# Decoder step with sparse attention: TensorE's order around its waits in the sample stage, and who copies and pads

## The reference

```python
# per sample: 2048 past rows of k and v, 4 kv heads of 64, 4 query heads per kv head, 4 tokens
kc, vc = compress(rows)                      # blocks of 32 rows, stride 16, through a small MLP; keys normed + rotary
s_c = einsum('qhgd,nhd->hgqn', q, kc)        # scores against the 127 compressed blocks
p_c = masked_softmax(s_c);  o_c = p_c @ vc
imp = p_c @ overlap                          # importance of each block of 64 rows
top = top_k(imp + forced, 16)                # the blocks each head and token may read
p_s = masked_softmax(q @ k_sel, top);  o_s = p_s @ v_sel        # 2048 selected-branch rows
p_w = masked_softmax(q @ k_win);       o_w = p_w @ v_win        # last 512 rows
o   = g_c * o_c + g_s * o_s + g_w * o_w
```

## Time and profile before

| | |
|---|---|
| Median of three runs | 2348.47 us (2348.05 to 2349.93) |
| The profiled execution | 2348.25 us, span 2346.6 us |
| TensorE busy, whole span | 2095.6 us (89%) |
| Sample stage | 1676 to 2268 us of the span, 592 us |
| TensorE busy in the sample stage | 494.51 us, mean granted clock 0.90 |
| One sample, second and third | 72.72 and 74.01 us |

### The profile page before, as it was taken

How to read it: one execution, slowest core, us unless ns; L and a number is a source line. 1 busy time by engine, 2 the same in 40 slices (tenths; PEclk the granted TensorE clock), 3 DMA queues, 4 the chain that set the end, 5 groups by cost and what they waited for, 6 DMA issues and landing times. The chain is left out here.

```text
span 2346.6 us, 25998 instructions
## 1 busy us (share of the span) xinstructions
PE 2095.6 (89%) x9553; PEld 1219.1 (52%) x9553; DVE 730.6 (31%) x1535; ACT 480.8 (20%) x1063; POOL 213.9 (9%) x325
## 2 busy tenths in 40 slices
PE   6998999999999999889899986787788887888878
PEld 3225545554664654468533675454454554545547
DVE  2012323322323232301213404555343233432342
ACT  1111211211121121100200122444322222222220
POOL 0000010010010001000000001323310101101000
PEclk9998999999999999889999987878889988899889
DMA  6862362343146136242122543000223442233420
GB/s 177 277 217 108 125 225 83 125 168 137 73 180 214 39 137 228 102 156 71 36 72 55 150 153 118 1 1 1 90 100 133 161 161 89 98 134 161 126 73 38
DMA packets 118889, 281.22 MB, mean 120 GB/s; under 512 B 33112, under 2 KB 41758, under 8 KB 115335
## 3 DMA queue, kind: packets, MB, share of 16 engines
q1 hardware_dynamic: 100636, 170.56, 22.0%
q0 software_dynamic: 12928, 109.54, 11.6%
q10 hardware_dynamic: 5268, 0.36, 0.2%
HBM read 227.78 MB, written 60.86 MB: 123 GB/s over the span
## 5 line engine op out<-in xcount | busy, mean ns | idle before, releaser
L1483 PE MATMUL sample_bank<-area 128*128 128x508 f32 x512 | 221.3, 590 | 0.0
L1296 PE MATMUL proj_bank<-stage,area 128*128 128x512 f32 (+1 forms) x400 | 175.6, 600 | 6.3 <-ACT area L1358 6.3
L1021 DVE SCALAR_TENSOR_TENSOR mlstm_cring<-mlstm_cring,mlstm_cur_old,mlstm_bank 128x512 f32<-128x512 f32 x128 | 87.1, 744 | 223.4 <-PE mlstm_bank L787 223.4
L1483 PEld LDWEIGHTS sample_bank<-area 128*128 128x128 f32 x512 | 96.0, 190 | 114.7 <-issue 114.7
L1261 PE MATMUL proj_bank<-area,stage 128*128 128x272 f32 x512 | 119.1, 396 | 20.6 <-DMA area<-act_scratch 20.6
L1296 PEld LDWEIGHTS proj_bank<-stage,area 128*128 128x128 f32 (+1 forms) x400 | 69.7, 176 | 111.7 <-issue 110.2
L705 PE MATMUL mlstm_bank<-h,stage 128*128 128x272 f32 x512 | 120.2, 397 | 7.6 <-SPq L593 7.6
L760 PE MATMUL mlstm_bank<-h,stage 128*128 128x272 f32 x512 | 121.2, 395 | 0.0
L1261 PEld LDWEIGHTS proj_bank<-area,stage 128*128 128x128 f32 x512 | 98.3, 192 | 41.2 <-issue 20.7
L771 PE MATMUL mlstm_bank<-stage,h 128*128 128x512 f32 x256 | 114.1, 599 | 0.0
L705 PEld LDWEIGHTS mlstm_bank<-h,stage 128*128 128x128 f32 x512 | 98.2, 192 | 28.2 <-DVEq L940 7.7
(11 more groups left out here) (468 smaller groups left out, 2761.4 us busy)
## 6 DMA issues: line engine op xcount, KB each, us to landing
stage<-in_a_w_in SPq DMA_DIRECT2D x16, 2048.0 KB, 9.2
mlstm_cring<-in_state_C SPq DMA_DIRECT2D x32, 1024.0 KB, 5.6
o_Cs<-mlstm_cring POOLq DMA_DIRECT2D x32, 1024.0 KB, 4.7
stage<-in_a_ada_w SPq DMA_DIRECT2D x6, 2048.0 KB, 8.0
stage<-in_b_ada_w SPq DMA_DIRECT2D x6, 2048.0 KB, 8.2
stage<-in_kv_ada_w SPq DMA_DIRECT2D x4, 2048.0 KB, 7.9
stage<-in_a_w_out SPq DMA_DIRECT2D x4, 2048.0 KB, 8.9
sample_winr<-in_cache_kv_win SPq DMA_DIRECT2D x8, 1024.0 KB, 5.4
```

The lines of the kernel that those rows point to most:

```text
L1021: dve.scalar_tensor_tensor(c, c, cur_old[:, n:n + 1], bank[:, b_big("outer", n * KH + k), :], ALU.mult, ALU.add).then_inc(E["c_new"], 1)
L1296: last = pe.matmul(o[0:rows, :], h[:, k, at:at + rows], w[:, k, :], start=(k == 0), stop=(k == KD - 1))
L1483: last = pe.matmul(bank[:, 3, 0:n].rearrange("p (h m) -> p h m", h=BKV), w1[:, c, s * 8 + k, :], xt[:, k, :, s:s + M - 1], start=(k == 0 a ...
```

## The change

Five edits, all in `phase_sample`:

- TensorE turns the last key chunk before it waits for the compressed keys, not after their transposes.
- `score(2)` stands before the wait for the window's exponentials instead of after the compressed output.
- The selected values are formed in two halves, tiles 0 to 7 after `pd_ok` alone, tiles 8 to 15 after `p_ok`.
- `v_used` is gone: `pv_mm` starts at one, and SyncE and GpSimd wait for it; TensorE no longer waits for itself.
- GpSimd copies all eight pieces (`piece_d` and `last_piece` are gone); the padding of the queries is VectorE's (`zero_ok` is gone).

The diff, cut to its core:

```diff
 # SyncE
-                sp.wait_ge(E["v_used"], n + 1)
+                sp.wait_ge(E["pv_mm"], n + 1)
                 sp.dma_start(winr[:, :, :], win_src[bass.ds(n, 1)].rearrange("o p a c -> p (o a) c")).then_inc(E["win_in"], 16)
...
 # GpSimd
-            pool.memset(qz_all[:, :, :, :], 0.0)
...
                     if f == BKV - 1:
-                        hold(pool, E["v_used"], n + 1, E["pass_pool"])
+                        hold(pool, E["pv_mm"], n + 1, E["pass_pool"])
                         load_blocks(pool, I, S, "cache_kv_sel", flat(sel[:, :, :], "pac"), E["sel_in"])
-                    if f % BKV == BKV - 1:
-                        continue
                     if f >= 3:
                         hold(pool, E["xt_tr"], n * 16 + 2 * (f - 2), E["pass_pool"])
...
-                    hold(pool, E["piece_d"], n * 2 + 2, E["pass_pool"])
                     load_blocks(pool, I, S, "cache_kv_cmp", S.stage[:, :], E["rows_in"])
...
 # TensorE
-                    if h == BKV - 1:
-                        pe.wait_ge(E["piece_d"], n * 2 + c + 1)
-                    else:
-                        pe.wait_ge(E["piece_ok"], n * (2 * BKV - 2) + c * (BKV - 1) + h + 1)
+                    pe.wait_ge(E["piece_ok"], n * (2 * BKV) + f + 1)
...
                 last.then_inc(E["new_mm"], 1)
+                turn_keys(4)
                 pe.wait_ge(E["kc_done"], n + 1)
...
                 last.then_inc(E["kct_tr"], 1)
-                turn_keys(4)
                 pe.wait_ge(E["kct_ok"], n + 1)
...
+                score(2)
                 hold(pe, E["exp_ok"], n * 5 + 1, E["pass_pe"])
...
                 last.then_inc(E["oc_mm"], 1)
-                score(2)
...
                 pe.wait_ge(E["pd_ok"], n + 1)
+                values(0, range(8))
                 pe.wait_ge(E["p_ok"], n * 2 + 2)
-                values(0).then_inc(E["pv_mm"], 1)
-                pe.wait_ge(E["pv_mm"], n + 1)
-                pe.sem_inc(E["v_used"], 1)
+                values(0, range(8, NT[0])).then_inc(E["pv_mm"], 1)
...
 # VectorE
-            dve.wait_ge(E["zero_ok"], 1)
+            dve.memset(qz_all[:, :, :, :], 0.0)
+            dve.drain()
+            for pr in range(2):
+                for h in range(2):
+                    lo, at = h * BD, h * G * TS_
+                    for g in range(G):
+                        dve.tensor_copy(qz_all[lo:lo + BD, :, pr, at + g * TS_:at + (g + 1) * TS_],
+                                         S.qs[lo:lo + BD, pr, g, :].rearrange("p (n t) -> p n t", n=NS))
...
-                dve.wait_ge(E["pv_mm"], n + 1)
+                dve.wait_ge(E["pv_mm"], n + 2)
```

More of the change, by code:

```diff
@@ L1928, in phase_sample @@
         bank = ps("bank", [P, 8, 512])
-        names = (COMPRESS_SEMS + """ next_in rows_in sel_in win_in rows_used piece_d v_used zero_ok qz_ok kct_tr kct_ok cs_mm
+        names = (COMPRESS_SEMS + """ next_in rows_in sel_in win_in rows_used  qz_ok kct_tr kct_ok cs_mm
             cs_max cs_exp cs_ok pct_tr pct_ok imp_mm imp_ok group_mm hide_ok k_tr k_a k_d sc_mm sc_ok new_mm max_ok exp_ok
@@ L1969, in _ @@
             sp.wait_ge(E["rows_used"], NS)
-            sp.wait_ge(E["piece_d"], NS * 2)
             w = I["b_w_out"][0].rearrange("(a h g d) n -> h a d g n", a=2, h=2, g=G)
@@ L1981, in _ @@
         def _(pool):
-            pool.memset(qz_all[:, :, :, :], 0.0)
-            pool.drain()
-            for pr in range(2):
-                for h in range(2):
-                    lo, at = h * BD, h * G * TS_
-                    for g in range(G):
-                        pool.tensor_copy(qz_all[lo:lo + BD, :, pr, at + g * TS_:at + (g + 1) * TS_],
-                                         S.qs[lo:lo + BD, pr, g, :].rearrange("p (n t) -> p n t", n=NS))
-            pool.drain().then_inc(E["zero_ok"], 1)
             def of_sample(n, next_rows):
@@ L2024, in _ @@
             ident = C("ident")
-            pe.sem_inc(E["v_used"], 1)
+            pe.sem_inc(E["pv_mm"], 1)
             pe.sem_inc(E["pieces_used"], 1)
@@ L2102, in _, with values @@
                 last.then_inc(E["oc_mm"], 1)
-                score(2)
-                def values(br):
+                def values(br, tiles):
                     first = NT[0] if br == 1 else 0
-                    for t in range(NT[br]):
+                    for t in tiles:
                         v = winr if br == 1 else sel
@@ L2111, in values @@
                                       v[:, t, values_of(0, pr)], start=(t == 0), stop=False)
+                    if t < NT[br] - 1:
+                        return
                     for pr in range(2):
@@ L2119, in _ @@
                 pe.wait_ge(E["p_ok"], n * 2 + 1)
-                values(1)
+                values(1, range(NT[1]))
                 hold(pe, E["oc_ok"], n + 1, E["pass_pe"])
@@ L2194, in keys_out @@
                     dve.tensor_copy(keys_t(i)[:, 1, :], bank[:, key_bank(2 * i + 1), :]).then_inc(E["k_d"], 1)
-                def last_piece(c):
-                    f = c * BKV + BKV - 1
-                    dve.tensor_copy(pieces[:, f % 3, :].rearrange("p (a d) -> p a d", d=BD),
-                                    rows[:, :, f * BD:(f + 1) * BD]).then_inc(E["piece_d"], 1)
                 dve.tensor_copy(qz[:, :, :], qz_all[:, bass.ds(n, 1), :, :].rearrange("p o a r -> p (o a) r"))
                 dve.drain().then_inc(E["qz_ok"], 1)
-                compress_dve(dve, E, n, M, xt, kcv, ss, tmp, S.kg0, C, bank, between=keys_out,
-                             last_piece=last_piece)
+                compress_dve(dve, E, n, M, xt, kcv, ss, tmp, S.kg0, C, bank, between=keys_out)
                 keys_out(3)
```

## The result

The changed kernel takes 2360.91 us as the median of five runs (2358.48 to 2362.72), the kernel before beside it 2348.60 us: a ratio of 1.0051 (95% interval 1.0036 to 1.0065). It is slower by some 12 us where 15.5 us of gain were forecast, and the time lies outside the range of the prediction. The profiled execution took 2360.91 us, 12.66 us more than the one of before.

A forecast was written before the change was run, and what follows sets the result against it. TensorE was taken to set the pace, with its idle time and low clock to win. Gains of 0.6 + 4.5 + 6.9 + 0.7 + 2.8 = 15.5 us took 2348.25 to 2332.75 us; range 2323 to 2343.

The forecast's parts named there:

- part 5: All pieces copied by GpSimd, query padding on VectorE: 2.8 us of gain, bounds -2 and 3.4.
- Cost: nothing: GpSimd's two extra pieces per sample: the fourth hidden under the window's wait, the eighth under turning; no cost.
- part 4: One semaphore for values done: SyncE issues the window's transfer 0.1 us earlier, seven times, 0.7 us of gain.
- Part 1: Last key chunk turned before the compressed-keys wait: 0.07 us, eight times, 0.6 us of gain; bounds 0 and 8.6.
- Part 2: Second selected chunk's scores before the window's exponentials: VectorE's score waits vanish, 4.5 us of gain; bounds 2.5 and 6.5.
- Part 3: First half of selected values runs under ScalarE's copy of turned weights: 6.9 us of gain; bounds 3 and 6.9.
- Part 5's padding: Query padding moved to VectorE at the stage's start, freeing GpSimd 3.4 us earlier: 2.8 us of gain.
- The bounds of the sum: Range of the likeliest forecast's whole time, said to include 4 us of clock either way: 2326 to 2340 us.
- The late fourth piece: Rival: GpSimd cannot copy while its gather is prepared, compress products start 1 to 2 us late; about 2345 us; chance 0.04.
- The falling clock at the window's wait: Rival: a merged TensorE gap of about 1.5 us before the compress products lowers the clock; 2364 us; chance 0.04.

The follow-up runs named there:

- pieces alone: Kernel before with GpSimd copying all eight pieces, nothing else changed: 2349.75 us, ratio 1.0004.
- order alone: Kernel before with TensorE's three reorderings only (early key chunk, early scores, values in two halves): 2338.46 us, ratio 0.9960.
- signal back: Changed kernel with `v_used` restored, all pieces still GpSimd's, padding still VectorE's: 2335.53 us, ratio 0.9939.
- signal alone: Kernel before without `v_used`, VectorE still copying its two pieces and GpSimd padding: 2348.87 us, ratio 1.0001.
- fourth piece back: Changed kernel with the fourth piece copied by VectorE again, the eighth still by GpSimd: 2336.04 us, ratio 0.9944.
- fourth piece later: Changed kernel with GpSimd's fourth piece held until both halves of the second piece are turned: 2335.29 us, ratio 0.9940.
- fifth piece later: Changed kernel with GpSimd's fifth piece held for one half-piece more: 2345.37 us, ratio 0.9988.
- padding back: Changed kernel with the query padding (memset and 16 copies) on GpSimd again: 2362.45 us, ratio 1.0047.
- reduction in the copy's place: Changed kernel with VectorE's per-sample query copy written as a reduction over an axis of length one: 2340.14 us, ratio 0.9952.
- the last run: Changed kernel with all query copies as reductions and the next window load released by the window's own value products: 2332.05 us, ratio 0.9923.

## Why the prediction was wrong

**The step that failed** is part 5, "Cost: nothing" for the pieces in the loop; the cover that it named, the wait for the window, hid the pieces but not what they did to another instruction. The boundaries were put at 0.7 us of gain and lost 20.7. I asked when the fourth piece would be ready for TensorE and never asked what VectorE does while GpSimd copies. The harm came only together with part 4, whose side effect was missed.

What the runs show, worked out from the rows of GpSimd and VectorE in the seven boundaries of each kernel:

| Kernel | copy starts after gather's start | copy takes | copy's end |
|---|---|---|---|
| before, pieces alone, order alone, signal back | 0.51 to 0.52 | 0.17 to 0.18 | within the gather |
| signal alone, fourth piece back, fourth piece later | 0.61 to 0.62 | 0.34 to 0.35 | 0.00 to 0.01 after the gather's |
| fifth piece later | 0.61 to 0.62 | 1.44 to 1.45 | 0.06 after one piece |
| changed kernel, padding back | 0.61 to 0.62 | 2.42 to 2.43 | 0.06 after two pieces |
| reduction in the copy's place | 0.61 to 0.62 | 0.20 to 0.21 | within the gather |

With `v_used`, VectorE is released by the last product itself and GpSimd a tenth of a microsecond later, by the signal; without it by the same event. So the copy starts at 0.52 us into the gather or at 0.61. Where the fourth piece may not start yet (second row), the copy at 0.61 waits to the gather's end, 0.17 us, and that is all that the tenth is seen to cost. Where the piece may start, the copy waits through the pieces behind the gather as well.

That it is the waiting piece which makes the wait long is seen also at the stage's start, where the padding copies fall into the first gather at smaller steps. Here is the run with the later fourth piece:

```profile
1681.07 1.05 POOL L1549 DMA_INDIRECT sample_sel<-in_cache_kv_sel,blk  x1 [0.16 <-issue]
...
1681.49 0.17 DVE L2177 COPY x<-qs 64x32 f32<-64x32 f32 x1
...
1681.67 0.43 DVE L2177 COPY x<-qs 64x32 f32<-64x32 f32 x1
```

Copies that start 0.33 and 0.41 us into the gather run freely, and the one at 0.59 waits to the gather's end. In the changed kernel, where the first piece is already turned when that gather starts, the copy at 0.33 us takes 2.79 us, as shown above; it takes the same 2.79 us with the signal back, and 1.82 with the later fifth piece. So the edit of part 5 puts a piece behind the gather and the edit of part 4 lets it start before the copy is done: together they make the wait 2.2 us long. In the kernel before there is a pause of 0.95 us between gather and pieces, and the copy is through before.

This is the rule that the prediction cited in part 5, of the Trainium skill (SBUF — State Buffer, section "SBUF: two separate sides"): VectorE's copies within SBUF and GpSimd's instructions share a port pair, one holds it for a whole instruction, the other waits. Beside the stage's first pieces the trace agrees with it: the copies waited to 0.03 us after the piece. Behind a gather it goes further than the rule: a copy of 0.176 us took 2.42, through the rest of the gather and two pieces, and the measurement decides. The same page says under "Who interferes with whom" that a reduction never contends on trn2, and here it takes 0.20 us at that place. What the runs show is that place and form decide; that a port is the reason is the page's account. I applied the rule to the 16 paddings, which run once, and not to the copy of the same kind that runs in every sample. The row that should have warned me, the one query copy of 0.596 us, I used as a price for the padding only.

**What the stall costs.** In the boundary shown, TensorE takes 7.88 us from its first transpose to the window's (1831.32 to 1839.20); with the signal back it is 5.15 us. A part is the clock, in the windows view of TensorE alone (busy, then granted clock), first the 16 transposes before the stall, then the 16 after it, then the 16 after the next boundary's stall:

```profile
1831.32:1833.31 1.99, 1.99 (x18) 1.00 0.22 63
1836.28:1839.40 3.12, 3.12 (x17) 0.60 0.84 360
1909.31:1912.98 3.67, 3.67 (x17) 0.50 1.00 430
```

After a wait of 2.96 to 2.98 us the engine was granted 0.50 to 0.64 of full speed in all seven boundaries: the lower of its two levels, or a mean between the two. With the later fifth piece, after 1.99 or 2.00 us of waiting, it was granted 1.00 in three boundaries and 0.52 to 0.79 in four; the second and the fourth of them:

```profile
1830.45:1832.44 1.99, 1.99 (x17) 1.00 1.29 427
...
1975.30:1978.89 3.59, 3.59 (x18) 0.52 1.18 497
```

So the length of this one wait does not tell the clock behind it.

**Parts 1 to 3 held.** Part 1: -1.4 us where 0.6 of gain was put. Part 2: -4.6 against 4.5, and VectorE's waits for scores are gone as foretold. Part 3: -7.2 against 6.9. Together 13.2 us by stages and 10.3 as the measured total of the three alone. That part 2 hit its number is partly luck: in the traces that have the new order its stage takes 9.45 to 10.02 us, a gain of 2.6 to 7.2 us.

**Part 4's size** is too small to be told: the gap of 0.67 us at the end of a sample is gone, and where nothing else holds the boundary it is 6.49 to 6.59 us instead of 6.63, 0.04 to 0.14 less where 0.1 was put. But with all pieces GpSimd's and the signal kept it is 6.58 us. The window's transfer takes the rest, as argued; the last run, which loads it earlier, shows it by the 1 us that then goes.

**Part 5's padding** was put at a gain of 2.8 us with -2 as the bound; it lost 2.4. Neither price of a copy, 0.18 or 0.6 us for each of the 16, is what happened, so that the bound by the higher one comes near is luck. Twelve copies ran at the lower price. Three waited for a piece, some 2.2 us in all, near the 3 us that the prediction worked out from the rule. The fourth waited 2.6 us, through the gather and two more pieces, where the prediction let GpSimd "pause for its gather" and counted nothing.

**The bounds of the sum.** The lower one, 2326, takes in the 4 us of clock, the upper one, 2340, leaves them out; with them it is 2332.75 + 2 + 4.8 + 4 = 2343.55. The measured time lies above either.

**The rivals.** The late fourth piece was the reverse of what happened: the piece came at once behind the gather, and a later one is faster by 25 us. The falling clock at the window's wait comes near in number (2364 us), not in mechanism: the clock fell, but behind VectorE's late copy and in the transposes, and the window's wait had gone.

**What stays open**: why a copy that waits behind a gather stays behind two pieces, while beside pieces alone it gets in after one; and whether a copy at 0.52 us into the gather would be held if the fourth piece might start by then. No run has that pair, and no row shows when GpSimd takes the port.

## What to carry to other kernels

Before work is moved to GpSimd, list VectorE's copies within SBUF that may fall beside it, however small, and ask what stands behind each: the price is not the copy but the piece, or behind a gather all the pieces, that it waits for, and then the engine that waits for VectorE. Where such a copy must stay, a reduction over an axis of length one, or a deliberate pause of GpSimd behind the gather, took the loss away here. And edits that cost nothing each can cost a per cent together, when one puts work behind a gather and the other lets it start sooner: test them in pairs.

## What was not expected of the hardware

- VectorE's copy, once it waited in a gather, did not get in between the gather and two pieces of 1.04 us each (2.42 us), though it was there 0.33 us before the first of them. Beside pieces alone the copies got in after one piece (0.78 to 1.01 us).
- The gather alone held it too, for 0.17 us (0.346 instead of 0.176 us), when it started 0.61 us into it; one that started at 0.41 us ran freely.
- A stall of 2.97 us on TensorE brought a granted clock of 0.50 to 0.64 in what followed; one of 1.99 us left it at 1.00 in three boundaries and brought 0.52 to 0.79 in four.
